# The front stage of a one-core transformer block: how its planner prices the weight loads, and where the first keys and queries of the next stage are loaded

## The reference

```python
x = x + 0.5 * rms_norm(swiglu(rms_norm(x, ffn1_pre_g), ...), ffn1_post_g)
h = rms_norm(x, mix_pre_g)
proj = h @ w_in                                   # 1024 x 3096: attention part and recurrent part
rwkv_cols = rwkv_cols + (prev - rwkv_cols) * rwkv_mu
o_nsa = nsa_mixer(...)      # compressed keys and values, selected blocks, window of 512, rotated queries and keys
o_rwkv = rwkv7_mixer(...)   # recurrence over 8 heads with decay, rate, bonus and gate
x = x + rms_norm(concat([rms_norm(o_nsa, nsa_out_g), o_rwkv]) @ w_out, mix_post_g)
h, m = rms_norm(x, mem_pre_g), rms_norm(mem, mem_kv_g)      # mem: 256 tokens
x = x + rms_norm(memory_cross_attention(h, m, wq, wk, wv, wo), mem_post_g)
x = x + 0.5 * rms_norm(swiglu(rms_norm(x, ffn2_pre_g), ...), ffn2_post_g)
```

## Time and profile before

| | us |
|---|---|
| median of three runs | 2806.92 |
| the profiled execution, own time | 2805.54 |
| its span | 2803.8 |
| PE busy in the span | 2668.0 (95%) |
| DVE busy | 1756.8 (63%) |
| ACT busy | 966.5 (34%) |

### The profile page before, as it was taken

One profiled execution on the slowest core, in us unless ns is written; L12 is line 12 of the kernel. 1 busy time (PEld: TensorE's weight loads), 2 busy tenths in 40 slices (PEclk: granted clock), 3 DMA queues, 4 the chain that ended last, 5 costly groups with the idle time before them and its releaser, 6 DMA issues. The chain is left out here.

```text
span 2803.8 us, 47405 instructions
## 1 busy us (share of the span) xinstructions
PE 2668.0 (95%) x19368; PEld 2201.6 (79%) x19368; DVE 1756.8 (63%) x2869; ACT 966.5 (34%) x1731; POOL 87.9 (3%) x121
## 2 busy tenths in 40 slices
PE   6999999999799999799999996999997999999998
PEld 5888887887577788788888885877776888887887
DVE  5766665777544464477777776653445765666676
ACT  4322222213433343344444444343432322222122
POOL 0000000000000000111111110000000000000000
PEclk9999999999899999899999998999998999999999
DMA  4221223224422377611111112530121222213224
GB/s 140 83 83 63 86 86 112 90 99 152 121 90 83 113 240 202 163 44 38 34 36 36 29 40 66 176 128 8 47 97 57 86 86 90 86 62 133 90 90 158
DMA packets 230633, 260.91 MB, mean 93 GB/s; under 512 B 63426, under 2 KB 186560, under 8 KB 230464
## 3 DMA queue, kind: packets, MB, share of 16 engines
q1 hardware_dynamic: 228880, 256.91, 28.7%
q10 hardware_dynamic: 1584, 1.60, 0.2%
HBM read 189.17 MB, written 64.06 MB: 90 GB/s over the span
## 5 line engine op out<-in xcount | busy, mean ns | idle before, releaser
L715 PE MATMUL f_ps<-hi,f_wh 128*128 128x512 f32 x768 | 301.6, 393 | 19.2 <-DVE f_wl L501 11.9
L717 PE MATMUL f_ps<-hi,f_wl 128*128 128x512 f32 x768 | 300.3, 391 | 0.0
L715 PE MATMUL f_ps<-f_t1h,f_wh 128*128 128x512 f32 x480 | 187.1, 390 | 0.0
L716 PE MATMUL f_ps<-f_t1l,f_wh 128*128 128x512 f32 x480 | 186.8, 389 | 0.0
L715 PEld LDWEIGHTS f_ps<-hi,f_wh 128*128 128x128 f32 x768 | 145.2, 189 | 52.5 <-issue 10.7
L2091 PE MATMUL fr_dense_ps<-hi,fr_wh 128*128 128x512 f32 x400 | 167.2, 418 | 7.2 <-DVE fr_wl L2385 7.2
L717 PEld LDWEIGHTS f_ps<-hi,f_wl 128*128 128x128 f32 x768 | 145.1, 189 | 30.3
L715 PE MATMUL f_ps<-f_t2h,f_t3h 128*128 128x512 f32 x384 | 150.8, 393 | 8.4 <-DVE one_y L607 4.1
L2093 PE MATMUL fr_dense_ps<-hi,fr_wl 128*128 128x512 f32 x400 | 156.7, 392 | 0.0
L2092 PE MATMUL fr_dense_ps<-one_lo,fr_wh 128*128 128x512 f32 x400 | 156.7, 392 | 0.0
L716 PE MATMUL f_ps<-one_lo,f_wh 128*128 128x512 f32 x384 | 150.6, 392 | 0.0
(11 more groups left out here) (423 smaller groups left out, 6389.9 us busy)
## 6 DMA issues: line engine op xcount, KB each, us to landing
one_y<-in_w_in SPq DMA_DIRECT2D x25, 512.0 KB, 4.3
f_raw<-in_ffn_w_gate SPq DMA_DIRECT2D x11, 1024.0 KB, 5.4
f_raw<-in_ffn_w_up SPq DMA_DIRECT2D x11, 1024.0 KB, 7.8
act<-one_y SPq DMA_DIRECT2D x44, 256.0 KB, 2.0
f_raw<-in_ffn_w_down SPq DMA_DIRECT2D x11, 1024.0 KB, 4.9
f_raw<-act SPq DMA_DIRECT2D x11, 1024.0 KB, 4.9
early<-in_ffn_w_gate SPq DMA_DIRECT2D x11, 1024.0 KB, 5.4
early<-in_ffn_w_up SPq DMA_DIRECT2D x11, 1024.0 KB, 7.8
```

What stands on the lines that cost most here:

```text
L715: nc.tensor.matmul(out, wh, xh, start=start, stop=False)
L716: nc.tensor.matmul(out, wh, xl, start=False, stop=False)
L717: return nc.tensor.matmul(out, wl, xh, start=False, stop=stop)
```

## The change

Three things are edited. In `front_plan` the event `landed` is gone; `load` itself now costs SP 0.2 us instead of 0.5 us and is 5.0 us late, and since each `load` needs the one before it, the plan now places two loads at least 5.2 us apart. `load_w1` 1 is 7.0 us late instead of 14.0 us. In the code of `load`, the five `lead` calls no longer stand behind the last load: one stands behind each of the loads 33 to 37.

```diff
-        event(("load", c), "sp", 0.5, *free, c and ("load", c - 1))
-        event(("landed", c), "pool", 0.0, ("load", c), late=4.8)
-        event(("w_hi", c), "act", 1.1, ("landed", c), c and ("w_hi", c - 1), c >= 2 and ("mm", c - 2, 1))
+        event(("load", c), "sp", 0.2, *free, c and ("load", c - 1), late=5.0)
+        event(("w_hi", c), "act", 1.1, ("load", c), c and ("w_hi", c - 1), c >= 2 and ("mm", c - 2, 1))
...
-    event(("load_w1", 1), "sp", 0.2, ("hid", 0), late=14.0)
+    event(("load_w1", 1), "sp", 0.2, ("hid", 0), late=7.0)
...
-                if c == CHUNKS - 1:
+                if c == CHUNKS - 8:
                     sp.wait_ge(multiplied, PROJECTED)
-                    for which in (("queries", 0), ("keys", 0), ("keys", 1), ("queries", 1), ("queries", 2)):
-                        lead(sp, *which)
+                if CHUNKS - 8 <= c < CHUNKS - 3:
+                    lead(sp, *[("queries", 0), ("keys", 0), ("keys", 1), ("queries", 1), ("queries", 2)][c - CHUNKS + 8])
```

## The result

| | before | after |
|---|---|---|
| median of the runs | 2806.97 us (2805.54 to 2810.27) | 2832.43 us (2830.89 to 2833.32) |
| span of the profiled execution | 2803.8 | 2829.7 |
| last copy of a memory key starts | 1143.04 | 1171.05 |
| PE begins the next stage | 1154.4 | 1177.1 |

The change makes the kernel slower by the ratio 1.0085 [1.0072, 1.0099], some 24 us. The forecast was 2816, with a range up to 2826. Its direction and both its places were right, its size was not.

The account below looks back on a forecast made before the run. PE was taken to bound the front stage. Late weight 4.0, clock 1.0 and stage end 4.1 sum to 9.1 us, which on the median 2806.9 gave 2816, range 2806 to 2826.

Parts of the forecast that it names:

- both its places: Front stage: losses at `hid` 1 in the middle and at the memory products of chunks 36 to 40 at the end.
- The weight of the second turn: Middle of front stage: second compression weight lands late behind four stores, so `hid` 1 starts 3.0 to 4.3 us late; 4.0 taken.
- the bytes are the same and the engines have a backlog all this time, so whichever is last of the five lands at about 1046: Middle: last of four stores and the second weight lands about 1046, so `hid` 1 starts between 1045.2 and 1046.5, not 1042.2.
- up to 1.3 less: Middle: the four stores and the weight, all issued by 1036, might at best drain 1.3 us faster.
- The clock: PE's lower clock after two or three stalls in the front stage: 0 to 1.4 us each, 1.0 taken in all.
- one stretch that was cut off too early: First feed-forward: 4.13 us PE idle, mean granted clock 0.63, 2.7 us busy, so the low clock cost about 1.4 us.
- The end: End of front stage: last product 7.3 us late behind late loads, 3.2 us gained at the last store; net 4.1.
- the chain: Chunks 36 to 40, load to product, each load awaiting an earlier result: late by 2.7, 5.3, 6.0, 6.0, 7.3 us.
- 12 us for the keys' bytes in my upper bound: Full-backlog case at the end: 2.5 MB of queries and keys ahead of load 36 take 12 us at 213 GB/s.
- the clock falls again and again: Rival: PE at 1.2 GHz through the last five products, priced 6 us, and longer at the weight's stall; 2824, chance 0.14.
- The upper bound of 8.5 net: End of stage with full backlog ahead of loads 36 and 37: last product 11.7 us late, net 8.5.
- 4.3 at least: Weight loads of 512 KB in this stage take 4.3 us or more to land, against 3.2 by the skill's rule.

Follow-up runs that it names:

- e1: Kernel before, plan unchanged, with the five query and key lead calls moved behind loads 33 to 37; 2815.93 us, ratio 1.0026.
- e2: Kernel before with only the second compression weight's lateness in the plan set to 7.0 instead of 14.0; 2819.70 us, ratio 1.0034.
- e9: Changed kernel with the second weight issued ahead of the rotated stores and the five leads back behind the last load; 2823.39 us, ratio 1.0052 to kernel before.
- e4: Kernel before with the second weight's lateness 7.0, but SP issuing that weight ahead of the four rotated stores; 2808.66 us, ratio 0.9996.
- e5: Kernel before with the second weight's lateness 7.0 and 56 extra matmuls ahead of the weight wait at `hid` 1; 2824.56 us, ratio 1.0056.
- e10: Kernel before with the second weight's lateness 7.0 and 28 extra matmuls ahead of the weight wait at `hid` 1; 2817.84 us, ratio 1.0033.
- e6: Changed kernel with SP issuing the second weight ahead of the four rotated stores; 2824.34 us, ratio 1.0051 to the kernel before.
- e8: Kernel before, plan unchanged, with all five query and key lead calls moved behind the last store of km; 2819.86 us, ratio 1.0036.
- e11: Kernel before with two of the three query groups (eight transfers of 128 KB) moved behind the last store of memory keys; 2805.71 us, ratio 0.9991.
- e7: Kernel before, old plan, with only the two key lead calls moved behind loads 34 and 35; 2810.58 us, ratio 0.9998.

## Why the prediction was wrong in size

**What held.** Nothing but the front stage moved. `hid` 1 waits for its weight, chunks 36 to 38 and 40 wait for their loads, which are issued one by one, and the boundary gets shorter. e1 (early leads), e2 (late weight) and e9 (late loads) show that each part alone is a loss: 7.3, 9.5 and 14.6 us by their ratios. These do not add up to the 24 of the change, they are 7 us more. Leads at the end of a late row of loads lengthen the boundary, which e9 pays and the changed kernel does not.

**The weight of the second turn: 4.0 forecast, 7.5 measured.** The failed step is "the bytes are the same and the engines have a backlog all this time, so whichever is last of the five lands at about 1046". Before, the five transfers went from 1031.22 to 1046.5, in 15.3 us. After, the first is issued at 1033.02, since it is now a store whose data has to be ready, while the weight could have gone 1.8 us earlier. By then there was no backlog: that first store landed in 2.7 us, before in 9.5, and the DMA share of 1032 to 1036 is 0.87, before 1.13 by the same view:

```profile
1032.00:1036.00 4.00, 4.00 (x20) 3.29 (x19) 4.00 (x5) 3.84 (x6) 0.00 (x0) 1.00 1.13 285
```

From there to the last landing it is 16.6 us, 1.3 us more where I had taken up to 1.3 less; the cause of these 1.3 us stays open. The landings came in the order of issue (the last store landed in 6.7 us, at 1041.4), so that the warning of the Trainium skill (DMA: Bandwidth & Descriptors, Queues, rings and completion order) that a later transfer may overtake an earlier one did not show in this place. e4 shows the place in the queue to be the cause.

**The clock: 1.0 forecast in all, 2.8 measured at `hid` 1 alone.** I had scaled one stretch that was cut off too early. It ends at 476 us, and the clock was still low behind it:

```profile
476.00:480.00 4.00, 4.00 (x14) 3.19 (x13) 3.22 (x5) 0.00 (x0) 0.00 (x0) 0.71 0.70 262
```

By PE's timeline the matmuls there start 0.43 us apart up to 478.16 and 0.23 us apart from then on. Twelve of them took 5.2 us in place of 2.7, so that stall had cost 2.5 us and not the 1.4 that I took as its upper bound. Here the wait was 7.1 us, and 64 matmuls in a row came right behind it while the clock was at 1.2 GHz. e5 and e10 bring `hid` 1 back to 7.3 and 7.4 us without touching its transfer.

**The end: 7.3 late and 3.2 back forecast, 17.7 late and 5.3 back measured.** With the shift of 10.3 taken off, the chain compares so:

| chunk | issue forecast | issue measured | landing forecast | landing measured |
|---|---|---|---|---|
| 36 | 1122.2 | 1122.3 | 6.9 | 13.1 |
| 37 | 1127.7 | 1133.4 | 6.9 | 9.0 |
| 38 | 1131.2 | 1139.7 | 6.9 | 6.5 |
| 39 | 1136.7 | 1144.3 | 4.3 | 4.0 |
| 40 | 1140.8 | 1151.2 | 4.3 | 4.0 |

The landing of 36 is the first failed number of the chain. I had 12 us for the keys' bytes in my upper bound and took 6.9 for the value, from loads that had no keys in front. The keys delay load 35 as well, and the first queries load 34, both of which the chain took to be in time. The cast of 35 holds up ACT, and with it the copies of chunk 34 and of `vm`; the queries behind load 36 hold up SP until 1142.48. Both stand ahead of load 37, 5.7 us later than forecast. The two causes are of nearly one size there (`vm` is copied at 1141.3), and no run separates them. From 39 to 40 the delay grows once more, by 2.8 us: the product of 37, cast at 1152.78 and copied at 1160.66, takes 7.9 - 2.3 = 5.6 us with the clock at 0.50 instead of 2.9 us, and load 40 waits for the store of 37. The product of 35 took as long (cast at 1139.04, copied at 1146.93), and its store stands ahead of load 38. The prediction had priced that rival ("the clock falls again and again", 2824) only as slower products; it missed that a slow product also issues the next load late. The upper bound of 8.5 net for this term was passed as well: 12.4. The gain at the boundary was larger than forecast, since the last store landed in 1.7 us behind an emptied queue, where I had taken the 3.0 of the earlier trace rows.

The rule of the Trainium skill (DMA: Bandwidth & Descriptors, Anatomy of one DMA), by which such a load takes an estimated 3.2 us, is fitted there to transfers that GpSimd issues; these are issued by SP. No load of this stage's weights meets it: the shortest takes 3.8 us before and 3.7 after, so the prediction's "4.3 at least" was a median and not the least. Other loads of 512 KB come close to it: four of `mem_wo` in the tail have a median of 3.3 us in the kernel before. Those are read in rows of 4 KB, this stage's weights in runs of 512 bytes; whether that is the reason was not tested.

**What stays open.** How the 17.7 us split between keys' bytes, SP's blocked issuing and the clock is not fully told apart. Late loads without early leads cost the products 9.2 us (e9), and early leads add 9.3 to that (e6). Early leads under the old plan cost 13.1 (e1), so the two overlap. The clock is inside all of these; no run held it up in the memory products.

## What to carry to other kernels

When an order moves a transfer behind others, work out its landing from when the first of them can be issued, not from a backlog that is taken as given. In a chain in which a load is issued only after an earlier result, each lateness comes back: in the landing, in the engine that waits in line, and in the slow clock after the wait; start the chain at the first transfer behind the moved bytes, not at the first one that waits for a store. When the price of a slow clock is read from an earlier stall, follow the row until the clock is back. And the issuing engine's own time for many small transfers belongs to the path of whatever it must still do.

## What the runs showed of the hardware

- Issuing takes the issuing engine longer when much is still under way ahead. Two transfers of 128 KB took SP 1.3 us in e8 and e11, and up to 8.21 us in e1, behind loads and keys of 512 KB each. SP in e1, then in e7, in which five loads took it 18 us; a single such load took 0.38 us at 1154.55 in the changed kernel:

```profile
1118.75 8.21 SPq L1071 DMA_DIRECT2D hi<-rot_hi  x2
```

```profile
1115.58 18.24 SPq L1935 DMA_DIRECT2D fr_six<-in_mem_wk  x5
```

- The same load of 512 KB landed in 4.0 to 13.6 us within 40 us of one execution (the changed kernel), the long ones right behind the keys.
- A float32 matmul of 126 columns is two instructions in the trace: 56 written ones were 112, in 12.66 us.
